# Seven products for eight in two chunks of five FFN contractions, on one core of Trainium2

## The reference

```python
def swiglu(x, w_gate, w_up, w_down):
    return (jax.nn.silu(x @ w_gate) * (x @ w_up)) @ w_down

h = h + 0.5 * swiglu(rms_norm(h, ffn1_norm[i]), ffn1_w_gate[i], ffn1_w_up[i], ffn1_w_down[i])
```

## Time and profile before

| | us |
|---|---|
| median of 3 runs | 1742.56 |
| lowest, highest | 1741.95, 1742.88 |
| profiled execution | 1742.88 |
| its span in the profile | 1741.1 |

### The profile page before, as it was taken

The page is one execution under the profiler, slowest core; times in us unless marked ns, Lnnn a source line. Parts: engine busy times, 40 slices in busy tenths (PEclk is TensorE's granted clock), DMA queues, the critical chain, the costliest instruction groups (busy, mean ns, idle before and its releaser), DMA issues.

```text
span 1741.1 us, 24237 instructions
## 1 busy us (share of the span) xinstructions
PE 1728.5 (99%) x9535; PEld 1499.9 (86%) x9535; DVE 1262.9 (73%) x1602; ACT 1002.9 (58%) x1245; POOL 59.2 (3%) x95
## 2 busy tenths in 40 slices
PE   9999999999999999999999999999999999999998
PEld 8888998888888888888888888888888988888887
DVE  6766777766677666876667898867666898876665
ACT  6544657644467444754457866464446965565444
POOL 7200000000000000000001000000000000000000
PEclk9999999999999999999999999999999999999999
DMA  7755535665555655465645554356555554446552
GB/s 244 243 190 191 170 122 169 215 218 192 193 169 177 210 186 183 138 207 188 192 145 189 186 169 145 122 185 219 191 193 170 160 180 132 138 166 213 189 185 89
DMA packets 211564, 311.65 MB, mean 179 GB/s; under 512 B 6434, under 2 KB 166112, under 8 KB 211360
## 3 DMA queue, kind: packets, MB, share of 16 engines
q1 hardware_dynamic: 207472, 303.84, 53.1%
q0 software_dynamic: 3712, 6.44, 1.3%
q10 hardware_dynamic: 304, 0.33, 0.1%
HBM read 309.54 MB, written 1.05 MB: 178 GB/s over the span
## 4 chain that ended last, share of the span: by engine, by line
PE 91%; ACT 4%; DVE 3%; issue 1%; DMA 0%; SPq 0%; DVEq 0%; ACTq 0%
PE psD L1942 28%; PE psA L1831 27%; PE psA L1836 14%; PE psA L1909 3%; PE psA L1924 3%; PE psA L1775 3%; PE psA L1942 2%; PE psD L2228 2%; PE psA L1928 1%; PE psA L1913 1%; PE psA L1780 1%; PE psA L2012 1%; ACT hi L455 1%; PE psD L2165 1%; PE psD L2012 1%
## 5 line engine op out<-in xcount | busy, mean ns | idle before, releaser
L924 DVE TENSOR_TENSOR lo<-raw,hi 128x2048 fp32r<-128x2048 f32 x285 | 650.6, 2290 | 171.1 <-ACT hi L455 170.2
L455 ACT ACTIVATE hi<-raw 128x2048 fp32r<-128x2048 f32 x285 | 542.5, 1909 | 77.0 <-PE psD L1942 33.6
L1831 PE MATMUL psA<-xT,hi 128*128 128x512 f32 x2094 | 501.1, 390 | 0.1
L1831 PEld LDWEIGHTS psA<-xT,hi 128*128 128x128 f32 x2094 | 387.2, 188 | 76.9 <-DVE xT L957 0.3
L1836 PEld LDWEIGHTS psA<-xT,lo 128*128 128x128 f32 x2112 | 271.9, 191 | 11.8 <-issue 0.5
L1836 PE MATMUL psA<-xT,lo 128*128 128x256 f32 x2112 | 276.8, 283 | 0.1
L1942 PE MATMUL psD<-hi,prod_hi 128*128 128x512 f32 x544 | 173.6, 393 | 1.3 <-issue 1.3
L1942 PE MATMUL psD<-hi,prod_lo 128*128 128x512 f32 x544 | 171.9, 390 | 0.0
L1942 PE MATMUL psD<-lo,prod_hi 128*128 128x512 f32 x544 | 142.3, 389 | 0.0
L593 ACT ACTIVATE scr<-psA 128x512 f32<-128x512 f32 x66 | 39.4, 596 | 165.5 <-PE psA L1836 165.5
L608 ACT ACTIVATE prod_hi<-scr 128x512 fp32r<-128x512 f32 x66 | 41.7, 632 | 157.8 <-DVE scr L1306 157.8
(11 more groups left out here) (306 smaller groups left out, 1912.3 us busy)
## 6 DMA issues: line engine op xcount, KB each, us to landing
raw<-in_w_in SPq DMA_DIRECT2D x48, 1024.0 KB, 5.2
raw<-in_ffn_w_up SPq DMA_DIRECT2D x43, 1024.0 KB, 5.3
raw<-in_ffn_w_gate SPq DMA_DIRECT2D x43, 1024.0 KB, 5.4
raw<-in_ffn_w_down SPq DMA_DIRECT2D x43, 1024.0 KB, 4.9
raw<-in_w_gate SPq DMA_DIRECT2D x22, 1024.0 KB, 5.4
raw<-in_w_up SPq DMA_DIRECT2D x22, 1024.0 KB, 5.3
raw<-in_w_down SPq DMA_DIRECT2D x22, 1024.0 KB, 4.9
raw<-in_lru_w_in SPq DMA_DIRECT2D x10, 1024.0 KB, 5.3
```

The lines of the kernel that those rows point to most:

```text
L455: act.activation(hi[:, n % RING, :], raw_of(n), ACT.Copy).then_inc(hi_ready, 1)
L924: dve.tensor_tensor(lo[:, n % RING, :], raw_of(n), hi[:, n % RING, :].bitcast(F32), ALU.subtract).then_inc(lo_ready, 1)
L1831: pe.matmul(psA[:, bank + f, :], w_hi[:, k, f * P:(f + 1) * P], xT[:, k].rearrange("p e s -> p (e s)"), start=(k == 0), stop=False)
```

## The change

In chunks 7 and 8 of FFNs 1 to 5 the down product is regarded as a two-by-two block product: 2 token tiles by 2 row blocks of features, times 2 row blocks by 2 halves of D. Eight block products are replaced by seven, of sums and differences of blocks (the scheme is Strassen's, in Winograd's form with shared sums). The units of such a chunk are two: the first with four weight blocks (128 x 2048), the second with three (128 x 1536), so that each of these FFNs has 35 units for 33. Every product is still three terms: 12 and 9 matmuls.

- SP loads the chunk's rows into space of their own in the scratch area, just after ups(7) and ups(8), and not in the ring.
- GpSimd makes the weight sums: one 128x512 in place (`first_sum`), three more (`sums_ready`). It makes the sums of the product's blocks, features by tokens: four of 128x256 (`prod_sums`), each waiting for the one before by a semaphore.
- DVE writes the product into a "tall" tile of seven blocks of 128; ACT rounds all seven in one (128x896), DVE takes the low part in one.
- Order on PE: gates and ups of 7, 8 and 9 without a down unit between; then for each of the two chunks the two seven-units; then down(6); then a wait for `parts_summed`; then gates(10), ups(10), and the last two contractions as before.
- Of the seven products, three are added straight into their output in `psD`. Four (M1, M5, M7, M6) are summed over the two chunks in the four banks of `psA`, which gates and ups used before. ACT copies one bank out, and DVE joins them in four sums, three of them in a row (`parts_joined`, ahead of the split of ups(10) in its queue). Later, ahead of `gate_sum` of chunk 10, it adds the four results times the factor to `h` (`parts_added`).
- `raw_of`, `landed_at` and the like count the ring's units apart from the seven-units. The loop has two turns for four in these FFNs, and chunk 6 is written out.

The core of the diff (blank lines left out):

```diff
@@ gpsimd @@
+                        def first_sums(k):
+                            w = view(raws[k % len(raws)], 4, 512)
+                            pool.wait_ge(seven_landed[k % len(raws)], 16 * seven_count[f, k])
+                            pool.tensor_tensor(w[:, 1, :], w[:, 1, :], w[:, 0, :], ALU.subtract).then_inc(first_sum, 1)
+                        def other_sums(k):
...
+                            pool_add(to[:, 0, :], w[:, 3, :], w[:, 1, :], ALU.subtract)
+                            pool.tensor_tensor(to[:, 1, :], to[:, 0, :], w[:, 0, :], ALU.subtract).then_inc(sums_ready, 1)
+                            pool.tensor_tensor(to[:, 2, :], w[:, 2, :], to[:, 0, :], ALU.subtract).then_inc(sums_ready, 1)
+                        def prod_sums(k):
+                            x = tall(f, k)[2].rearrange("p (m s) -> p m s", m=7)
+                            pool.wait_ge(seven_prod, seven_before[f] + k + 1)
+                            pool_add(x[:, 5, :], x[:, 0, :], x[:, 1, :], ALU.subtract)
+                            pool_add(x[:, 1, :], x[:, 1, :], x[:, 3, :], ALU.add)
+                            pool_add(x[:, 4, :], x[:, 1, :], x[:, 0, :], ALU.subtract)
+                            pool.tensor_tensor(x[:, 6, :], x[:, 2, :], x[:, 4, :], ALU.subtract).then_inc(seven_summed, 1)
+                        for k in range(q):
+                            if k < len(raws):
+                                first_sums(k)
+                            if k < len(wides):
+                                other_sums(k)
+                            prod_sums(k)
@@ scalar @@
+                        for c in range(m + 1, CH - 1):
+                            split_to(n)
+                            gate_half(n + 1)
+                            n += 1
+                            split_to(n)
+                            silu(c0 + c, c)
+                            if c > m + 1:
+                                seven_high(c - m - 2)
+                            up_half(n + 1)
+                            n += 1
+                        for k in range(q):
+                            split_to(n)
+                            if k == 0:
+                                prod_high(p0 + m + 1, CH - 2, (m + 1) % 2)
+                            n += 1
+                            split_to(n)
+                            n += 1
+                        act.wait_ge(block_used, n)
+                        act.activation(parts(f)[:, 0, :], psA[:, 0, :], ACT.Copy).then_inc(parts_out, 1)
+                        split_to(n)
+                        n += 1
@@ vector @@
+                    def parts_joined(n):
+                        u = parts(f)
+                        dve.wait_ge(parts_out, sum(1 for g in SEVEN if g <= f))
+                        dve.wait_ge(block_used, n)
+                        for to, bank, x in ((1, 3, 0), (2, 2, 1), (3, 1, 1), (4, 1, 2)):
+                            if to in (2, 4):
+                                dve.wait_ge(parts_summed, 4 * seven_nth + to - 1 - (to == 4))
+                            dve.tensor_tensor(u[:, to, :], psA[:, bank, :], u[:, x, :], ALU.add).then_inc(parts_summed, 1)
...
+                        for c in range(m + 1, CH - 1):
+                            split_to(n)
+                            if c > m + 1:
+                                seven_gated(c - m - 2)
+                            gate_sum(c0 + c, c)
+                            scaled_gate(c0 + c, c)
+                            n += 1
+                            split_to(n)
+                            up_sum(c0 + c, c)
+                            if c > m + 1:
+                                seven_low(c - m - 2)
+                            n += 1
+                        for k in range(q):
+                            split_to(n)
+                            if k == 0:
+                                multiplied(c0 + CH - 2, CH - 2)
+                            n += 1
+                            split_to(n)
+                            if k == 0:
+                                prod_low(p0 + m + 1, CH - 2, (m + 1) % 2)
+                            n += 1
+                        parts_joined(n)
+                        split_to(n)
+                        n += 1
                     for b in range(4):
                         if b < 2:
                             split_to(n)
                         if b == 0:
+                            if q:
+                                parts_added()
                             gate_sum(c0 + CH - 1, CH - 1)
@@ tensor @@
+                    def seven(n_at, n, k, products):
...
+                        pe.wait_ge(hi_ready, n_at)
+                        pe.wait_ge(seven_lo, seven_before[f] + k + 1)
+                        for to, x, w in products:
+                            own = to in (M1, M5, M6, M7)
+                            if own and k == 0:
+                                pe.wait_ge(up_summed if to in (M6, M7) else gate_summed, c0 + CH - 1)
+                            pe.matmul(bank(to), x_hi[:, x, :], w_hi[:, w, :], start=(own and k == 0), stop=False)
+                            pe.matmul(bank(to), x_lo[:, x, :], w_hi[:, w, :], start=False, stop=False)
+                        pe.wait_ge(lo_ready, n_at)
+                        for to, x, w in products:
+                            own = to in (M1, M5, M6, M7)
+                            last = pe.matmul(bank(to), x_hi[:, x, :], w_lo[:, w, :], start=False, stop=(own and k == q - 1))
+                        last.then_inc(block_used, 1)
...
+                        for c in range(m + 1, CH - 1):
+                            gates(n + 1, n, c0 + c)
+                            ups(n + 2, n + 1, c0 + c)
+                            n += 2
+                        for k in range(q):
+                            seven(n + 1, n, k, ((M1, 0, 0), (C11, 2, 2), (C12, 6, 3), (M5, 1, 1)))
+                            seven(n + 2, n + 1, k, ((C21, 3, 2), (M6, 4, 0), (M7, 5, 1)))
+                            n += 2
+                        down(n + 1, n, p0 + m + 1, m)
+                        n += 1
+                        nth = sum(1 for g in SEVEN if g < f)
+                        pe.wait_ge(parts_summed, 4 * nth + 4)
                     gates(n + 1, n, c0 + CH - 1)
                     ups(n + 2, n + 1, c0 + CH - 1)
```

More of the change, by code:

```diff
@@ L75 @@
 SCRATCH = 22784
+WIDE, TALL = 3 * 512, 7 * P
+SEVEN = {f: 2 for f in range(1, 6)}
+SEVEN_AT = {f: (8704, (12288, 14336), (16384, 17920)) for f in SEVEN}
+PAIR_LAST = CH - 3
 assert BAND + 2 * 2 * GT * 384 <= SCRATCH
@@ L431, in _ @@
         def _(act):
-            st = {"split": 0, "norm": 0, "updates": 0, "piece": 0, "ffn": 0, "step": 0, "rows": 0, "turned": 0, "gate": None, "gain": 0, "rstd": 0, "renorm": 0}
+            st = {"split": 0, "norm": 0, "updates": 0, "piece": 0, "ffn": 0, "prods": 0, "step": 0, "rows": 0, "turned": 0, "gate": None, "gain": 0, "rstd": 0, "renorm": 0}
             def step(ins):
@@ L910, in _ @@
         def _(dve):
-            st = {"split": 0, "norm": 0, "updates": 0, "piece": 0, "ffn": 0, "step": 0, "rows": 0, "update": None, "early": 2, "gain": 0, "rescaled": 0, "updated": 0, "renorm": 0, "between": None}
+            st = {"split": 0, "norm": 0, "updates": 0, "piece": 0, "ffn": 0, "prods": 0, "step": 0, "rows": 0, "update": None, "early": 2, "gain": 0, "rescaled": 0, "updated": 0, "renorm": 0, "between": None}
             def step(ins):
@@ new lines, in parts_added @@
+                    def parts_added():
+                        dve.wait_ge(parts_summed, 4 * seven_nth + 4)
+                        for t, c, at in ((0, 0, 0), (0, 1, 3), (1, 0, 2), (1, 1, 4)):
+                            step(dve.scalar_tensor_tensor(h[:, t, half_of[c]], parts(f)[:, at, :], col(FACTOR + t), h[:, t, half_of[c]], ALU.mult, ALU.add))
+                    seven_nth = sum(1 for g in SEVEN if g < st["ffn"])
+                    f, q = st["ffn"], SEVEN.get(st["ffn"], 0)
+                    m = PAIR_LAST - q
@@ L2112, in ups, with bank @@
                         feature_pairs(n_at, n, 2)
+                    def seven(n_at, n, k, products):
+                        w_hi, w_lo = (v[:, n % RING, :].rearrange("p (m d) -> p m d", d=512) for v in (hi, lo))
+                        x_hi, x_lo = (v.rearrange("p (m s) -> p m s", m=7) for v in tall(f, k)[:2])
+                        pe.wait_ge(hi_ready, n_at)
[11 more added lines that the diff above has]
+                        last.then_inc(block_used, 1)
+                    M1, M5, M7, M6 = range(4)
+                    C11, C12, C21 = range(4, 7)
+                    def bank(to):
+                        return psD[:, to - 4, :] if to >= 4 else psA[:, to, :]
                     feature_pairs(n + 1, n, 0, fresh=True)
@@ L2128, in _ @@
                         pe.wait_ge(cpos_exp, 1)
[L2129 removed]
+                    down(n + 5, n + 4, p0 + 1, 0, first=True)
                     n += 5
[L2131 removed]
```

(1 more changed line is left out.)

259 lines of the change are left out of this document (211 added, 48 removed).

## The result

The changed kernel takes 1752.81 us (median of 4 runs, 1751.18 to 1753.03) against 1742.49 for the kernel before on the same chip (4 runs, 1741.95 to 1742.88). The ratio is 1.0057, with a 95% interval of 1.0045 to 1.0069: 10.3 us slower, where 27.5 were forecast. The profiled execution took 1751.18, the shortest of the four.

What follows compares the result with a forecast made beforehand. PE was taken to bound the kernel. Per FFN, 2.65 us of waiting plus 4.2 of contention less 1.37 saved gave +5.5, or +27.5 over five FFNs: 1770.1 us from 1742.56, range 1747 to 1782.

Steps and rivals of the forecast that it cites:

- What bounds the kernel: PE, busy 99% of the span at full clock; only idle PE or a count of matmuls can change the time.
- Saved, 1.37 us an FFN: 21 matmuls for 24 in each of ten chunks: 0.684 us a chunk, 6.84 us in all, 0.39%.
- The walk: Queues from the end of ups(9) to gates(10), without contention: b1 0.2 late, its low part 0.4, joins 2.0; 2.65 us an FFN.
- Contention: GpSimd's sums against DVE in chunks 8 and 9, delaying PE: 4.2 us an FFN, bounds 0 to 5.2.
- The exclusion: A DVE step with two SBUF inputs and a GpSimd sum shut each other out; one earlier row showed DVE losing 0.63 us.
- the path: GpSimd's late sums delay ACT's rounding of the second tall product, then its ups copy, then b0's third product on PE.
- The signs named ahead: PE busy 6.8 us less, waits before b0, b1 and gates(10) in FFNs 1 to 5, longer or gapped splits beside GpSimd.
- Hidden edits: Updates of h before gate_sum(10), hidden with 1.9 us to spare, and the two early 1 MB loads: both priced at 0.
- No contention to speak of: Rival, 20%: GpSimd costs DVE nothing, leaving +1.28 us in each of five FFNs: 1749.0.
- A tie: Rival, 8%: waits of about 1.4 us an FFN: 1742.6.
- Still slower: Rival, 5%: GpSimd's sums cost more than priced or stall gate and ups units too; 10 us an FFN, 1792.
- Faster: Rival, 7%: DVE and ACT keep up after ups(9), joins ending within 16.4 us; with no wait at all 1735.7.

Runs made afterwards that it cites:

- e6: The faster version with joins and b1's rounding moved earlier, plus an eighth product in each second seven-unit (changes the output): 1746.15 us, 6.7 more for 30 matmuls.
- e4: Changed kernel with GpSimd writing zeros where it would form its sums, so the sums are left out: 1747.62 us, ratio 1.0030 to the kernel before.
- e7: Changed kernel with four more 128x128 GpSimd sums a chunk, repeats of two that are there: 1774.66 us, ratio 1.0187 to the kernel before.
- e5: e3 with the four updates of h moved on DVE from ahead of gate_sum of chunk 10 to behind product(10)'s low part: 1745.29 us.
- e3: Changed kernel with DVE's joins ahead of the split of gates(10) and ACT's rounding of product(9) behind b1's weights: 1739.48 us, ratio 0.9983 to the kernel before.
- e8: Changed kernel with one product (C12) left out of each first seven-unit, 30 matmuls less, output changed: 1754.15 us, ratio 1.0065 to the kernel before.
- e9: e3 with FFN 2's scaling of the pool's weights moved behind product(10)'s low part on DVE, ACT rounding product(10) before splitting them: 1742.37 us.
- e1: Changed kernel with DVE's joins moved ahead of its split of gates(10): 1746.89 us, ratio 1.0025 to the kernel before.

## Why the prediction was right in direction and wrong in size

- **What bounds the kernel.** Right. Nothing but PE's waits, its pace and its count moved the time, and the queues of ACT and DVE after ups(9) are where the cover ended.
- **Saved, 1.37 us an FFN.** Right as a count: e6 gives it back as 6.7 / 5 = 1.33. The prediction priced the new order at nothing and named 0.5 as the risk. It was 0.21 (42 matmuls x (0.2333 - 0.228)).
- **The walk, 2.65 of waiting.** The steps and their order were right, the sum 1.0 too high. Without contention (e4) it had b1 at 7.73, 0.2 late, and its low terms 0.4 late: measured 7.70, which at the slower pace is on time, and 0.29. Joins ending at 17.7: measured 16.9. The failed term is the chain of DVE instructions. It was added up from records that each overlap the next by 0.07 to 0.1 us (four joins are one row of 2.60, not 4 x 0.70; two splits one of 4.49, not 4.58), over a dozen instructions, which makes up 0.8. With PE at 15.27 rather than 15.05 the waiting is 1.7.
- **Contention, 4.2 of an expected 0 to 5.2.** This is the step that failed, and the larger one: 0.95 to 1.04 us an FFN (e4 against the changed kernel).
  The exclusion itself holds, in both directions. DVE's split at 437.15 began just behind a GpSimd sum and took 3.35, its 2.29 and 1.06 of the other's 1.30; the one at 442.72 took 3.19, the product at 445.83 1.78 for 0.69. GpSimd's sums at 438.43 and 443.73 took 3.23 and 3.35 beside splits, not 1.3. On this the Trainium skill ("SBUF — State Buffer", section "Who interferes with whom") says that the loser of the shared pair blocks for the whole instruction; no row of before showed that for GpSimd, and these rows agree with it for both engines to within 0.1 to 0.2 us.
  What was wrong was the load and the stretch. The product's sums are half as wide as I took them, about 0.45 us against 0.70. I set 7.05 us of DVE and 7.9 of GpSimd against the 11.1 of chunk 8, called the excess of 3.9 late, and let chunk 9 win nothing back, with 7.05 + 1.38 + 2.8 = 11.2 us of work in its 11.1. In the trace chunk 8 (428.94 to 440.08) has 6.0 us of DVE work with two SBUF inputs at the prices of the earlier trace rows, since the first product's low part (1.09) comes at 441.52, and GpSimd starts in it only at 434.56. Chunk 9 (440.08 to 451.21) has 6.5, since its second split is 128x1536, 1.76 for 2.29; with the second product's sums, 1.8, and DVE's two from PSUM, 1.4, that is 9.7 us, not 11.2. So there was room for what chunk 8 left over.
  Added up over the whole stretch, from the end of the first tall product (434.47) to the end of ups(9) (451.21), 16.7 us: DVE 9.5 with two SBUF inputs, GpSimd 9.2 (four sums of 1.28, eight of 0.45, and 0.5 of its own waits), 18.7 in all. That would have the last sum 2.0 late; it ended 0.28 late (451.49). So even this sum is too high; a part of each sum runs beside DVE (1.06 and 1.09 lost to sums of 1.30), and the rest of the 1.7 is not explained. What PE lost is more than 0.28, because ACT's rounding of the tall product (0.95) still stands between that sum and the ups copy: the copy starts 1.18 after ups(9) for 0.20 in e4, 1.0 late. No run separates the width of the sums from the stretch.
- **That the path was right and its load off** is shown by e7: with 3.6 us more of sums an FFN the very path of the prediction appears, b0's third product released by the ups sum, and the FFN gets 4.5 longer. The 27.5 forecast are between the changed kernel's 10.3 and e7's 32.4. In the changed kernel b0 doesn't wait at all; the ups copy is 1.0 late, which b0's third product still bears, and PE feels it first at b1.
- **The signs named ahead.** Waits before b1 and gates(10) in FFNs 1 to 5 and none in FFN 0, gates(10) released by a join, splits over 2.29 us beside GpSimd, its last sum after the end of ups(9): all seen. The wait before b0 and a PE busy sum less by 6.8 us (1.2 less) were not.
- **Hidden edits.** The updates of h are hidden, as said; e5 shows that their place matters. The loads are hidden in the changed kernel. Not foreseen: in FFN 2 the cover is thinner, 0.26 in the changed kernel, 1.16 to 1.56 once gates(10) comes on time.
- **The rivals.** *No contention to speak of* forecast 1749.0; e4, which has none, measured 1747.62. The changed kernel is 1.0 an FFN above it and far from the forecast's 4.2, so that rival was the nearer one. *A tie* (1.4 us of waiting an FFN) and *Still slower* (10 an FFN) didn't come: the waiting is 2.64. The rule of *Faster*, a joins' end within 16.4 us of the end of ups(9), held: e3 has them end 13.9 after it, and is faster. Its 1735.7 wasn't reached, for the most part by the pace (1.1 us) and by FFN 2 (1.2).

The direction had little to spare: without contention the walk said +1.28 an FFN, and 1.0 of that was waiting that didn't come. What was left, 0.3, shows as slower only together with the pace (0.21) and the restart (0.13), which the sum had at nothing; e4 is still slower than the kernel before (1.0030).

The sum with measured terms: waiting 1.7 + contention 0.95 - saved 1.37 + pace 0.21 = 1.5 an FFN, and 0.13 for the restart of gates(10).

## What to carry to other kernels

Before trading matmuls for sums on other engines, lay out the queue of each engine from the last unit that covers it to the first wait behind it, instruction by instruction: here the whole saving was 1.37 us an FFN, and two queue positions (a 0.63 us rounding ahead of a 1.48 us one, 2.6 us of joins behind a 2.3 us split) cost more than that. A wait that the change itself orders can often be placed before work that has slack, and that is worth trying before the change is given up. Where two engines exclude each other, set both loads against the whole stretch from the first input to the last use, take the sum for an upper bound (here 2.0 us late for a measured 0.3), and read the shapes of the operands twice.

## What the runs showed of the hardware that I had not expected

- The granted clock fell to the 1.2 GHz level for some us beside PE's waits of 1.67 us (e8), 1.99 (e5), 3.53 (e9, 0.65 on the mean from 709 to 712) and 3.59 to 3.61 (e7, all five FFNs). It stayed at 1.00 after waits of 0.73, 1.10, 1.16, 1.20 and 1.56 (e1, the row above), and in e8 after three of its five waits of 1.66 to 1.68. So the length of the wait alone doesn't decide. Matmuls then run 0.43 apart, for 0.23. What that costs depends on what comes next: in e7 and e8 nothing, since ACT and DVE set the next start; in e9 the way from FFN 2's a0 to FFN 3's a0 is 3.4 us longer than in e3, and only 2.4 of it is that its wait is longer (3.53 for 1.16).
- GpSimd and DVE take turns. A run of dependent 128x128 sums on GpSimd, each about 0.45 us alone, took 5.4 and 6.3 us for seven beside DVE's splits. GpSimd writing zeros (e4) held DVE up nowhere: its splits took 2.29.
- Matmuls of the same shape run at 0.2333 us in the seven-units and at 0.228 in the down units, at the same granted clock, and with eight products (e6) as with seven. What sets the difference stays open; the units differ in that they alternate between `psA` and `psD` and in the order of their terms, and neither was tried.
